# A hybrid decoder layer on eight cores: three barriered stages against an interleaved order with a transposed residual

## The chip, the cores and the metric

The kernel runs on the 8 cores of one Trainium2 chip. Each core computes one of the 8 sequences of the batch, 4096 tokens of 1024 channels, and no core talks to another. The time is that of the slowest core, in microseconds (us) on the device. Within a core, PE (TensorE) multiplies matrices, ACT (ScalarE) and DVE (VectorE) and POOL (GpSimd) do the elementwise work, and SP (SyncE) starts most of the DMAs; each engine works through its own instructions in a fixed order and waits on semaphores.

## What is computed

```python
h = rmsnorm(x, norm1_w); z = h @ w_in            # 1024 -> 5632 columns
q, k, v, xr, yr, ga, gr = split(z)               # 512 512 512 1024 1024 1024 1024
# A: 8 heads of 64; q and k normed; each query sees its own block of 256 keys (causal)
#    and the 3 past blocks whose mean key it likes best; bias by distance; softmax
o_attn = moba_attention(qh, kh, vh, rel_bias)
# B: conv over 4 tokens, then a gated linear recurrence over the sequence
xr = causal_depthwise_conv(xr, conv_w, conv_b)
hr = rg_lru(xr, ...)                             # r, i = sigmoid(block-diagonal 64x64)
o_rnn = hr * gelu(yr)
merged = sigmoid(ga + b) * (o_attn @ w_proj_attn) + sigmoid(gr + b) * (o_rnn @ w_proj_rnn)
x = x + merged @ w_out
x = x + square(relu(rmsnorm(x, norm2_w) @ w_ff1)) @ w_ff2
```

## The kernel before, in words

The kernel is written as a list of operations with the tiles that they read and write (class `Prog`). A planner gives every operation an estimated cost, plays the list through engine by engine, and writes out for each engine the order in which its instructions stand; semaphores follow from the tiles. `P.barrier()` cuts the list in three: behind a barrier every engine waits for all that came ahead of it, DMAs included, and the SBUF space (one arena) is laid out afresh. All instructions are issued from one line (L422), so groups of rows are told apart by their shapes. Tokens are worked in 8 chunks of 512 (`NCH`), each of 4 tiles of 128.

Stage 1 is q, k, v and attention. `frontend` norms a tile (square, Ln and Exp on ACT, one DVE pass) and transposes it on PE into hT. `FE(c)` multiplies hT with the q, k, v columns (24 matmuls of 128x512 a tile), norms q and k, and transposes them head by head. k of all heads (64 rows and 16 rows of block indicators) and v stay in SBUF. `GM(c)` scores each query against the key means of the blocks, takes the third largest with MAX8 and writes a mask of 0 or -30000 into 16 further rows of q, so that the score matmul adds it. `ATT(c, bl)` works on 256 queries of a head at a time: for each pair of key tiles two score matmuls (80x128 by 80x256), one Exp of 512 columns on ACT into PT, and four products with V (128x65). The order is attention of a chunk with `FE` and `GM` of the next put behind its first four heads. x, on SP, is loaded behind the table of biases, which goes through DRAM and back.

Stage 2 is everything from the RNN branch to the residual. Its weights (RNN input, gates, projections, output) are loaded by POOL DMAs that cast fp32 to bf16, and hT and the attention output come back from DRAM. `rnnA`, `rnnB`, `rnnC` are worked two column tiles at a time (`rnn_pair`): conv on DVE, two block-diagonal matmuls, Tanh and Exp and Sqrt on ACT, the scan on DVE, with GeLU built from Square, Tanh and two DVE passes. `rnn_pair` of chunk c+1 stands between the eight `gating` steps of chunk c, then comes the output projection with the residual, token-major, to DRAM.

Stage 3 is the MLP. All of its weights, 16 MB in bf16, are loaded into SBUF by POOL DMAs behind the barrier. `FEC` norms and transposes the tiles of a chunk with `frontend`; 32 groups of 8 matmuls with Relu (ACT) and a square (DVE or POOL) follow, then per token tile two groups of 32 matmuls for W2.

## Time and profile of the kernel before

| | us |
|---|---|
| median of 3 runs | 2813.45 |
| lowest, highest | 2812.91, 2818.64 |
| profiled execution: span of the slowest core | 2811.1 |
| spans of the 8 cores | 2786.8 to 2811.1 |
| PE busy | 2471.3 |
| ACT busy | 1581.7 |
| DVE busy | 1139.7 |
| POOL busy | 297.1 |

Busy time counts an engine's instructions without waits. The granted clock is the share of TensorE's full 2.4 GHz that it was given in a stretch; 1.00 is full, and 0.75 is a mix of its two levels, 2.4 and 1.2 GHz.

### The profile page before, as it was taken

Reading aid. Unit: us, or ns where it says so; the run is one execution under the profiler, and the core shown is the slowest. Engines: PE = TensorE matmul, PEld = TensorE weight load, DVE = VectorE, ACT = ScalarE, POOL = GpSimd, SP = SyncE. Lnnn points to the kernel's source line nnn. Section 1 sums busy time; section 2 is a strip of 40 time slices with the busy share of each in tenths; the row PEclk is TensorE's granted clock in tenths of the full one; section 3 lists DMA queues with packets and bytes.
Section 4 is the critical chain, followed back from the end, with each engine's and each line's share of the span. In section 5 each row is a group of like instructions: output and inputs, shape, how many; then the busy total and the mean of one; then the engine's idle time right before and its main releaser. Section 6 shows DMA issues by size and latency. Waiting matters only on the chain.

```text
span 2811.1 us, 48678 instructions; the slowest of 8 cores (2786.8 to 2811.1 us)
## 1 busy us (share of the span) xinstructions
PE 2471.3 (88%) x16534; PEld 1254.3 (45%) x16722; DVE 1139.7 (41%) x2276; ACT 1581.7 (56%) x2753; POOL 297.1 (11%) x279
## 2 busy tenths in 40 slices
PE   2778888889899746999999999956999999999999
PEld 0445655656565412444444444422444444444444
DVE  2565553342321135777777777321222122121221
ACT  0557867879799737888898889232122131231320
POOL 2000000000000012222222222120001010010110
PEclk9999989989999978999999999977999999999999
DMA  7111101010100194012211220297211211112111
GB/s 121 61 54 54 39 31 54 2 54 6 43 2 10 41 161 73 31 53 83 68 39 60 83 68 23 83 179 136 75 46 45 83 38 61 60 37 84 38 38 53
DMA packets 63373, 166.53 MB, mean 59 GB/s; under 512 B 6883, under 2 KB 27532, under 8 KB 60940
## 3 DMA queue, kind: packets, MB, share of 16 engines
q1 hardware_dynamic: 34428, 129.60, 14.2%
q0 software_dynamic: 28704, 33.82, 8.2%
q8 instruction: 139, 2.28, 0.3%
q14 instruction: 102, 0.84, 0.1%
HBM read 151.07 MB, written 46.15 MB: 70 GB/s over the span
## 4 chain that ended last, share of the span: by engine, by line
PE 78%; DVE 7%; ACT 5%; issue 5%; DMA 3%; another core or an unknown queue 1%; POOL 0%; DVEq 0%; ACTq 0%; SPq 0%; POOLq 0%
PE bank L422 78%; DVE arena L422 7%; ACT arena L422 5%; DMA arena<-w_in 1%; DMA arena<-x 1%; DMA arena<-out 1%; ACT L422 0%; DMA arena<-scr_w 0%; DMA arena<-pvec 0%; POOL arena L422 0%; DVEq L247 0%; DMA scr_w<-arena 0%; DMA out<-arena 0%; ACTq L247 0%
## 5 line engine op out<-in xcount | busy, mean ns | idle before, releaser
L422 PE MATMUL bank<-arena 128*128 128x512 bf16 (+8 forms) x16534 | 2471.3, 304 | 335.9 <-DVE arena L422 148.9
L422 PEld LDWEIGHTS bank<-arena 128*128 128x128 bf16 (+4 forms) x16722 | 1254.3, 100 | 1552.4 <-issue 572.1
L422 ACT ACTIVATE arena<-bank 128x512 bf16<-128x512 f32 (+2 forms) x1472 | 763.5, 781 | 694.9 <-PE bank L422 689.4
L422 ACT ACTIVATE arena<-arena 128x512 f32<-128x512 f32 (+4 forms) x578 | 343.8, 599 | 147.3 <-DVE arena L422 50.5
L422 DVE SCALAR_TENSOR_TENSOR arena<-arena 128x512 f32<-128x512 f32 (+2 forms) x321 | 278.5, 870 | 273.6 <-ACT arena L422 259.0
L422 DVE TENSOR_TENSOR arena<-arena 128x512 bf16<-128x512 f32 (+2 forms) x324 | 204.7, 632 | 327.5 <-ACT arena L422 318.1
L422 POOL TENSOR_TENSOR arena<-arena 128x512 bf16<-128x512 f32 x176 | 212.4, 1207 | 1177.1 <-ACT arena L422 457.3
L422 DVE TENSOR_TENSOR arena<-bank,arena 128x512 bf16<-128x512 f32 (+2 forms) x154 | 92.8, 621 | 372.4 <-PE bank L422 347.9
L422 ACT ACTIVATE arena<-bank,arena 128x512 f32<-128x512 f32 (+1 forms) x288 | 202.5, 733 | 62.5 <-PE bank L422 40.0
L422 DVE SCALAR_TENSOR_TENSOR arena<-arena,bank 128x512 f32<-128x512 f32 x256 | 171.9, 678 | 101.5 <-PE bank L422 62.0
L422 ACT COPY arena<-bank 128x1024 bf16<-128x1024 bf16 (+1 forms) x128 | 103.0, 805 | 186.0 <-PE bank L422 164.7
L422 ACT ACT_TABLE_LOAD x127 | 162.9, 1283 | 67.9 <-DVE arena L422 36.3
L422 DVE RECIPROCAL arena<-bank 128x1 f32<-128x1 f32 x256 | 33.5, 163 | 326.1 <-PE bank L422 325.1
L427 POOL DMA_DIRECT2D arena<-w_in x11 | 9.9, 920 | 956.9 <-DMA scr_o<-arena 956.0
L422 DVE TENSOR_REDUCE arena<-arena 128x16 f32<-128x1024 f32 (+1 forms) x47 | 73.1, 1555 | 71.0 <-ACT arena L422 71.0
L422 DVE TENSOR_TENSOR_SCAN arena<-arena 128x512 f32<-128x512 f32 x64 | 82.9, 1295 | 4.8 <-DVE arena L422 0.5
L422 DVE COPY arena<-bank 16x1024 bf16<-16x1024 bf16 (+3 forms) x97 | 57.8, 596 | 44.8 <-PE bank L422 44.2
L422 POOL TENSOR_SCALAR arena<-arena 128x512 f32<-128x512 f32 x64 | 43.1, 674 | 249.0 <-ACT arena L422 249.0
L422 DVE TENSOR_SCALAR arena<-bank,arena 128x64 bf16<-128x64 f32 x256 | 61.8, 279 | 2.4 <-DVE arena L422 0.6
L422 DVE COPY arena<-arena 128x3 f32<-128x3 f32 (+1 forms) x192 | 40.5, 211 | 50.5 <-ACT arena L422 34.0
L422 DVE SCALAR_TENSOR_TENSOR arena<-bank,arena 128x512 f32<-128x512 f32 x64 | 43.8, 685 | 29.3 <-PE bank L422 29.3
L422 ACT CAST arena<-arena 128x512 bf16<-128x512 f32 x64 | 39.2, 612 | 9.4 <-DVE arena L422 9.1
(18 smaller groups left out, 118.4 us busy)
## 6 DMA issues: line engine op xcount, KB each, us to landing
arena<-x SPq DMA_DIRECT2D x64, 512.0 KB, 4.2
out<-arena SPq DMA_DIRECT2D x64, 512.0 KB, 2.9
arena<-out SPq DMA_DIRECT2D x64, 512.0 KB, 4.3
arena<-w_ff POOLq DMA_DIRECT2D x16, 1024.0 KB, 77.0
arena<-w_in POOLq DMA_DIRECT2D x11, 1024.0 KB, 30.6
scr_h<-arena SPq DMA_DIRECT2D x8, 1024.0 KB, 4.9
arena<-scr_h SPq DMA_DIRECT2D x8, 1024.0 KB, 4.8
scr_o<-arena SPq DMA_DIRECT2D x8, 512.0 KB, 3.0
```

Of the source, the lines that this page charges most:

```text
L422: return P.add(eng, lambda e, m=meth, kw=kw: getattr(e, m)(**kw), reads, writes, cost=cost, fam=fam)
L427: return P.add(q, lambda e, kw=kw: e.dma_start(out=out, in_=in_, **kw), reads, writes, dsem=dsem, cost=(1200.0 if q == 'gpsimd' else 60.0) ...
```

## The change

The three stages are re-cut, the barriers go, and a new planner orders the whole program at once. The new planner takes at each moment, for each engine, the earliest-written operation that is ready by its own estimates; space is still laid out by stage, but an operation waits only for the users of the bytes that it takes over.

- Stage 1 is q, k, v alone. The reciprocal root of each norm is a power on POOL in place of Ln and Exp. q and k are transposed two heads at a time. hT, q, k and v are stored to DRAM, and the RNN and gate weights are loaded meanwhile, one load a tile.
- Stage 2 is the RNN branch, four column tiles at a time with GeLU in one instruction, with `GATE1` of the chunk before: both gates, the RNN projection, and its product with its gate. The attention gate (`t1_s`) and the gated RNN term (`rm_s`) go to DRAM in fp32. POOL DMAs cast the MLP weights from DRAM to DRAM into bf16 (`WCAST`).
- Stage 3 runs the rest. Attention works on 512 queries at a time, loads the keys and values of a head for each chunk (`KVLOAD`), and its units are spread between the dense units (gating, output projection, MLP) of the chunk before. MLP weights are re-read from DRAM in slabs of 1 MB for each chunk, four slabs deep. x and the result are held with channels on partitions (`xT`, `outT`, transposed on the host), so that the second norm is a column sum over ones on PE and needs no transposes. Scores have three PSUM banks, V products two, and all else three.

```diff
-            P.barrier()
+            if eng == "tensor":
+                nmov = fsize(kw["rhs"]) if "rhs" in kw else 128
+                c_ = max(nmov / 2.4 + 2.6, 28.0)
...
+                    if kw.get("op", None) == ALU.pow:
+                        c_ = nel * 135.0 + 800.0
...
+        load_x(0)
+        dma("sync", nw, nw_d, "c0b", [], ["nw"])
...
+        for j in range(3):
+            dma("gpsimd", wqkv[j], wqkv_d[j].rearrange("p (a b) -> p a b", a=8), "wqkv%d" % j, [], ["wqkv%d" % j])
...
+        abank = ring([1, 2, 3, 4, 5, 6])
+        hbank = ring([0])
+        tbank = ring([7])
...
+            op("gpsimd", "tensor_scalar", [sk], [sk], out=ssq[s], in0=ssq[s], scalar1=EPS, scalar2=None, op0=ALU.add)
+            op("gpsimd", "tensor_tensor", [sk, "mhalf"], [sk], out=ssq[s], in0=ssq[s], in1=mhalf, op=ALU.pow)
...
+        FEn(0)
+        for t in range(NT):
+            if t + 1 < NT:
+                FEn(t + 1)
+            FEq(t, FEm(t))
+            if t >= 4 and wB:
+                w_, src, nm = wB.pop(0)
+                dma("gpsimd", w_, src.rearrange("p (a b) -> p a b", a=8), nm, ["hT%d" % (t % NHT)], [nm])
+            if t == 6:
+                bias_table()
...
+        for s in range(NCH):
+            for g in range(2):
+                RNN(s, g)
...
+                if s > 0:
+                    for m in range(4 * g, 4 * g + 2):
+                        GATE1(s - 1, m)
+                RNN2(s, g)
+                if s > 0:
+                    for m in range(4 * g + 2, 4 * g + 4):
+                        GATE1(s - 1, m)
+                for _ in range(2):
+                    WCAST("orn:%d" % ((s * 8 + 4 * g) % NORN))
...
+        SB = [0, 1, 3]
+        OB = [2, 4]
+        DB = [5, 6, 7]
+        def gbank():
+            b = DB[gctr[0] % 3]
+            gctr[0] += 1
+            return b
...
+                        op("tensor", "matmul", ["kTr%d" % ks, "kTr%d:E" % ks] + qk, ["B%d" % sb], tag="S", out=bankf[sb][:, 0:nq],
+                           lhsT=kTr[ks][0:80, kt * 128:(kt + 1) * 128], rhs=qT[s][0:80, h, q0:CH], start=True, stop=bias is None)
...
+                        op("scalar", "activation", ["B%d" % sb], ["PT%d" % pi], out=PT[pi][:, 0:nq], in_=bankf[sb][:, 0:nq], func=AF.Exp, fam="expln")
+                        for qt in range(q0 // 128, 4):
+                            op("tensor", "matmul", ["PT%d" % pi, "Vr%d" % ks], ["B%d" % ob], tag="AV", out=bankf[ob][:, qt * 65:(qt + 1) * 65],
...
+                    dma("sync", t1r[r], t1_s[c, m], "t1r%d" % r, ["t1_s%d_%d" % (c, m)], ["t1r%d" % r])
+                    dma("sync", rmr[r], rm_s[c, m], "rmr%d" % r, ["rm_s%d_%d" % (c, m)], ["rmr%d" % r])
+                    b = gbank()
...
+                        op("tensor", "matmul", ["ss", "onesf"], ["B%d" % b2], tag="nrm", out=bankf[b2], lhsT=onesf, rhs=ss, start=True, stop=True)
...
+        extend(gating(0))
+        extend(outproj(0))
+        for c in range(NCH):
+            nx = c + 1 < NCH
+            extend(W1(c, 0))
+            extend(W2(c, 0))
+            extend(W1(c, 1))
+            w2 = W2(c, 1)
+            if nx:
+                marks[c + 1] = len(dense)
+                extend(gating(c + 1))
+                o_ = outproj(c + 1)
+                extend(o_[0:4])
+                extend(w2[0:4])
+                extend(o_[4:8])
+                extend(w2[4:8])
...
+            at = attention(c)
...
+            inject.setdefault(prev, []).append(lambda c=c: (QLOAD(c), GM(c)))
+            for i in range(prev, end):
+                acc += dense[i][0]
+                goal = tot * min(1.0, acc / (dt_tot * 0.92))
```

## Rows read from the trace of the kernel before

**Rows 1.** The page: span, and busy time of PE.

```profile
span 2811.1 us, 48678 instructions; the slowest of 8 cores (2786.8 to 2811.1 us)
...
PE 2471.3 (88%) x16534; PEld 1254.3 (45%) x16722; DVE 1139.7 (41%) x2276; ACT 1581.7 (56%) x2753; POOL 297.1 (11%) x279
```

**Rows 2.** Windows by stage: stretch, length, busy us (instructions), granted clock, DMA share, GB/s.

```profile
0.00:66.40 66.40, 10.64 (x19) 2.94 (x20) 13.26 (x16) 4.44 (x9) 17.01 (x8) 1.00 0.73 125
66.40:970.30 903.90, 786.36 (x8864) 495.52 (x8896) 357.80 (x1055) 705.00 (x1435) 0.00 (x0) 0.94 0.10 32
970.30:1110.70 140.40, 65.11 (x212) 23.79 (x217) 59.80 (x101) 73.84 (x102) 28.57 (x31) 0.73 0.80 137
1110.70:1825.90 715.20, 701.74 (x3175) 314.05 (x3240) 502.04 (x831) 566.17 (x791) 155.18 (x145) 1.00 0.18 58
1825.90:1960.20 134.30, 74.36 (x327) 33.04 (x332) 24.80 (x30) 36.91 (x67) 23.40 (x26) 0.75 0.96 165
1960.20:2811.10 850.90, 833.10 (x3940) 384.96 (x4020) 181.95 (x243) 195.38 (x350) 72.90 (x70) 1.00 0.16 54
```

**Rows 3.** Timeline of PE at the handovers: start, length, work, idle before and its releaser.

```profile
999.93 9.28 PE L422 MATMUL bank<-arena 128*128 128x512 bf16 x31 [29.66 <-DMA arena<-w_in]
...
1931.61 1.86 PE L422 MATMUL bank<-arena 128*128 128x512 bf16 x4 [6.78 <-DMA arena<-w_ff]
```

**Rows 4.** Timeline of DVE at the end: sums of output half tiles, 32 matmuls each.

```profile
2779.74 0.69 DVE L422 TENSOR_TENSOR arena<-bank,arena 128x512 f32<-128x512 f32 x1 [6.21 <-PE bank L422]
...
2807.37 0.69 DVE L422 TENSOR_TENSOR arena<-bank,arena 128x512 f32<-128x512 f32 x1 [6.21 <-PE bank L422]
```

**Rows 5.** Windows, columns as in rows 2: attention alone, late in its stage.

```profile
840.00:910.00 70.00, 67.71 (x874) 39.39 (x871) 9.10 (x44) 69.86 (x145) 0.00 (x0) 1.00 0.03 10
```

**Rows 6.** Timeline of PE: sixteen transposes in a row.

```profile
75.21 1.21 PE L422 MATMUL bank<-arena 128*64 128x128 bf16 x16 [1.47 <-DVE arena L422]
```

**Rows 7.** Groups by form, whole run: operation, shape, count, busy, mean ns, idle before.

```profile
L422 DVE MAX8 arena<-arena 128x8 f32<-128x16 f32 x208 | 36.6, 176 | 18.2 <-DVE arena L422 1.8
...
L422 PE MATMUL bank<-arena 128*128 128x512 f32 x8 | 8.2, 1127 | 27.8 <-DMA arena<-scr_w 27.8
...
L422 DVE TENSOR_TENSOR arena<-arena 128x128 f32<-128x128 f32 x26 | 7.5, 290 | 2.0
```

**Rows 8.** DMA issues: count, KB each, median us from issue to landing.

```profile
arena<-x SPq DMA_DIRECT2D x64, 512.0 KB, 4.2
out<-arena SPq DMA_DIRECT2D x64, 512.0 KB, 2.9
...
arena<-scr_h SPq DMA_DIRECT2D x8, 1024.0 KB, 4.8
...
arena<-w_proj_attn POOLq DMA_DIRECT2D x1, 1024.0 KB, 11.2
```

**Rows 9.** Groups by form, whole run: passes of the q, k, v stage, and POOL.

```profile
L422 POOL TENSOR_TENSOR arena<-arena 128x512 bf16<-128x512 f32 x176 | 212.4, 1207 | 1177.1 <-ACT arena L422 457.3 <-PE bank L422 396.5 <-DVE arena L422 323.3
...
L422 DVE SCALAR_TENSOR_TENSOR arena<-arena 128x1024 bf16<-128x1024 f32 x64 | 82.1, 1283 | 174.8 <-ACT arena L422 161.9 <-issue 12.9
...
L422 DVE TENSOR_TENSOR arena<-bank,arena 128x512 bf16<-128x512 f32 x64 | 41.2, 685 | 24.4 <-ACT arena L422 24.4
...
L422 DVE TENSOR_REDUCE arena<-arena 128x16 f32<-128x1024 f32 x32 | 38.9, 1217 | 52.1 <-ACT arena L422 52.1
...
L422 DVE TENSOR_REDUCE arena<-arena 64x8 f32<-64x2048 bf16 x15 | 34.2, 2278 | 19.0 <-ACT arena L422 19.0
...
L422 DVE COPY arena<-bank 64x1024 bf16<-64x1024 bf16 x32 | 21.8, 682 | 8.0 <-PE bank L422 7.9
```

**Rows 10.** Groups by form, PE in the attention stage (110.6 to 970.3): scores, V products.

```profile
L422 PE MATMUL bank<-arena 80*128 80x256 bf16 x2048 | 391.8, 282 | 14.4 <-ACT arena L422 11.0 <-DVE arena L422 2.2
L422 PE MATMUL bank<-arena 128*128 128x65 bf16 x4224 | 278.6, 196 | 18.1 <-ACT arena L422 9.1 <-DVE arena L422 2.8
```

**Rows 11.** Timeline of PE: the last V products of the attention stage.

```profile
966.33 0.28 PE L422 MATMUL bank<-arena 128*128 128x65 bf16 x4 [0.21 <-ACT arena L422]
```

More of the change, by code:

```diff
@@ new lines, in emit @@
+                if ds is not None:
+                    assert dq.setdefault(ds, e) == e
+                    dcount[ds] = dcount.get(ds, 0) + 16
+                    sig[i] = ("d:" + ds, dcount[ds])
+                elif has[i]:
+                    c += 1
+                    sig[i] = ("e:" + e, c)
+        names = sorted(set(s[0] for s in sig if s is not None))
+        pos = sorted(range(n), key=lambda i: (self.t0[i], i))
+        known = {e: {} for e in self.ENGS}
+        carried = [None] * n
@@ new lines, in emit @@
+        waits = [()] * n
+        for i in pos:
+            o = ops[i]
+            kn = known[o.eng]
+            want = {}
+            srcs = {}
+            for j in deps[i]:
+                if skip(j, i):
+                    continue
+                s, v = sig[j]
+                if v > want.get(s, 0):
+                    want[s] = v
+                    srcs[s] = j
+            w = []
+            for s in sorted(want, key=lambda s: -self.t1[srcs[s]]):
+                if kn.get(s, 0) >= want[s]:
+                    continue
+                w.append((s, want[s]))
+                kn[s] = want[s]
+                for s2, v2 in carried[srcs[s]].items():
+                    if v2 > kn.get(s2, 0):
+                        kn[s2] = v2
+            waits[i] = w
+            c = dict(kn)
+            own = "e:" + o.eng
+            if o.dsem is None and sig[i] is not None:
+                c[own] = sig[i][1]
+            carried[i] = c
@@ L364, in build_nc @@
     cG_d = dt_in("c_G", [33, 384])
[L365 removed]
+    cE_d = dt_in("c_E", [16, S], BF16)
     cm_d = dt_in("c_mtab", [128, 768])
[L367 to L371 removed]
@@ new lines, in build_nc @@
+        QLOAD(0)
+        GM(0)
+        dma("gpsimd", wpa, wpa_d.rearrange("p (a b) -> p a b", a=4), "wpa", [], ["wpa"])
+        dma("gpsimd", wo, wo_d.rearrange("p (a b) -> p a b", a=8), "wo", [], ["wo"])
+        at0 = attention(0)
+        for m in range(8):
+            for _, f in at0[m * 4:m * 4 + 4]:
+                f()
+            GATE1(NCH - 1, m)
+        for _, f in at0[32:]:
+            f()
+        for _ in range(3):
+            WLOAD()
+        dense = []
+        marks = {}
@@ new lines, in build_nc @@
+        inject = {}
+        prev = 0
+        for c in range(1, NCH):
+            end = marks[c]
+            at = attention(c)
+            tot = sum(w for w, _ in at)
+            dt_tot = sum(w for w, _ in dense[prev:end])
+            acc = 0.0
+            k = 0
+            inject.setdefault(prev, []).append(lambda c=c: (QLOAD(c), GM(c)))
+            for i in range(prev, end):
+                acc += dense[i][0]
+                goal = tot * min(1.0, acc / (dt_tot * 0.92))
+                while k < len(at) and (sum_ := sum(w for w, _ in at[:k])) < goal:
+                    inject.setdefault(i + 1, []).append(at[k][1])
+                    k += 1
+            while k < len(at):
+                inject.setdefault(end, []).append(at[k][1])
+                k += 1
+            prev = end
@@ L997, in build_nc @@
+        for i in range(len(dense) + 1):
+            for f in inject.get(i, ()):
+                f()
+            if i < len(dense):
+                dense[i][1]()
+        P.emit(nc, ["out%d_%d" % (c, dt_) for c in range(NCH) for dt_ in range(8)])
+        st.pop().close() if len(st) > 1 else None
+        build_nc.stats = (len(P.ops), P.n_sems, P.n_waits, P.end, {k: round(v / 1e3) for k, v in P.busy.items()}, pA_peak, pB_peak, p2_peak)
+        build_nc.prog = P
     return nc
 def _prep_inputs(inputs):
-    f = lambda a: np.ascontiguousarray(np.asarray(a, dtype=np.float32))
```

1661 lines of the change are left out of this document (812 added, 849 removed).

## Prediction

> **What bounds the kernel now.** I read the page first: TensorE is busy for 2471.3 of 2811.1 us [rows 1], so at most 340 us are idle, and a change that keeps its work can win little more than those. Then the busy time by stage, cut where the PE timeline shows the handovers [rows 2, 3]. The reader is to see three things there. The last two stages proper (RNN with gating, 1110.7 to 1825.9, and MLP, from 1960.2) hold PE busy for 701.7 of 715.2 and 833.1 of 850.9 us at a granted clock of 1.00: nothing is to be won in them. The attention stage leaves 903.9 - 786.4 = 117.5 us idle, at a clock of 0.94, so its work also runs slower than it could. And three stretches are mostly empty: the start (66.4 us, 10.6 busy), and the two handovers at the barriers (140.4 with 65.1 busy and 134.3 with 74.4 busy, at 0.73 and 0.75). In the first handover PE waits 29.7 us for weights, in the second 7 us at a time [rows 3]. Losses: 55.8 + 117.5 + 75.3 + 13.5 + 59.9 + 17.8 = 339.8 us.
>
> **What PE has to do afterwards.** A 128x512 matmul takes 27.63/128 = 0.2159 us (the four last output tiles, 2779.74 to 2807.37 [rows 4]). The change leaves their number: q, k, v 768, RNN input 1024, its gate blocks 128, merge gates 1024, the two projections 512 + 256, output 512, MLP 2048 + 2048; together 8320, 1796 us. Attention keeps its columns too: 67,584 score columns for each head before (256 queries at a time) and after (512 at a time, the four tiles on the diagonal 512 to 128 wide), plus 64,512 bias columns in all; 605,184 columns at 0.2159/512 are 255 us. The 4224 products with V stay. Their price comes from the end of the attention stage, where nothing else runs: 67.71 us of PE for 145 exps are 0.467 us for a pair of key tiles [rows 5], less 0.216 for 512 score columns, over four products: 0.063 us each, 265 us. Transposes fall from 1408 to 672 (q and k two heads at a time, masks all heads at once, no transposes ahead of the MLP because the residual is kept transposed): at 1.21/16 = 0.076 us [rows 6] 51 us. New are eight fp32 column sums over ones for the second norm, 1.127 us each by the fp32 row [rows 7], 9 us; 104 small block-score matmuls at not over 0.063 are 6.5. Sum: 2383 us at full clock.
>
> **Start.** Before, x sits on SP behind the bias table, and q starts at 66 us. After, x is the first load, and the bias table moves behind tile 6. What is late next is the weights of v, third on POOL's queue: a 1024 KB load there took 11.2 us when little else was queued [rows 8], so three are some 34 us; a few q and k matmuls fit ahead. Idle: 28 us.
>
> **Stage 1, q, k, v.** A tile is 24 x 0.2159 + 16 x 0.076 = 6.4 us of PE. DVE has 1.28 (norm) + 0.68 (copy of h) + 1.22 (two sums) + 2 x 0.69 + about 0.4 (q out) + half of a key sum, 2.28/4 = 0.57 [rows 9]: 5.5 us, just under. Ahead of the q and k scaling stands something new, a power on POOL (1 and 16 elements) in place of Ln and Exp on ACT, with two small adds. No POOL power is in the trace. From below it is free (hidden); from the other side the nearest POOL row, 512 elements in 1.21 us [rows 9], is far away; the change's own planner prices it at 135 ns an element plus 0.8, so 3.9 us a tile. Both hide under 6.4 us, and six banks let two tiles be in flight; I take 10 us of waits, and twice the planner's price, 7.8 us and the adds, would make POOL the bound at about 9 and cost 80 us. At the 0.94 of the old attention stage the 214 us of PE cost 14 more. The 22 weight loads moved onto POOL's queue stand one a tile behind these powers; they are needed only after the stage.
>
> **Stage 2, RNN and gates.** Step 0 has no gates of an earlier chunk beside it. Before, RNN of chunk 0 took 1110.7 - 999.9 = 110.8 us in four dependent pairs [rows 2, 3]; now there are two groups of four: about 56 us for 31 us of PE, 25 idle, and 10 more for its clock by the 0.73 to 0.75 of the handovers. The seven further steps have 336 matmuls, 72.5 us; the old stage lost 1.9% [rows 2], so 10 us over 508. ACT sheds one pass (GeLU in one instruction) and DVE two; not bound before, so worth nothing. The 128 new stores of gate terms stand on SP alone, hidden behind 508 us.
>
> **Into stage 3.** No barrier any more, and weights wait in DRAM as bf16, cast by POOL DMAs during stage 2. But the projection of chunk 7 waits for its last RNN chain, and it shares banks with attention of chunk 0: 18 us, against 59.9 before.
>
> **Stage 3.** 1053 us of dense matmuls and 540 of attention share PE. ACT has 0.482 us for an exp [rows 5], 1152 of them at most 555 us, and some 200 us of the rest: far from bound. DMA re-reads 16 MB of MLP weights a chunk, and at most 32 MB with keys, values, gate terms and x; at 1024 KB in 4.8 us [rows 8] that is under 154 of some 200 us, so hidden. Every score must go through exp before its V product, and PE works in order: in the old stage PE idled 14.4 + 18.1 us ahead of these two [rows 10]; I take 32 again, with 512-wide matmuls as better cover and a planner that knows the same latencies.
>
> One place I expect to wait: the seven chunk borders. All dense units, and the block mask of the next chunk, take banks 5, 6, 7 in one program-order ring. The mask (issued first) is a DVE chain of eight MAX8 at 0.176 and three passes at 0.29, 2.3 us and hops, so 10.5 us for four tiles [rows 7]. Behind it in the ring stand gating, output projection, and only then the second half of W2 that was put there as cover. Gating also waits on SP's reloads: two buffers, each round a load (under 4.2 us), 0.69 and 1.21 [rows 8, 9]. PE's other cover is the next chunk's attention, which needs the mask through eight more small DMAs on SP (landing as the 2.9 us store [rows 8], some 5.5 us with their issue). From the last W1 matmul: 10.5 - 3.5 (the mask starts two units early) + 5.5 - 3.5 (gating matmuls that fit) = 9 us each, 63 us. Bounds: 0 if attention of the old chunk is left over, and 30 us each if gating's four reload rounds (6.5 us each) stay bare too.
>
> **Tail**: 2811.1 - 2807.4 = 4 us as before [rows 1, 4].
>
> **Sum.** 2383 + 28 + 10 + 14 + 25 + 10 + 10 + 18 + 32 + 63 + 4 = 2597 us of span, against 2811.1. The median before is 2813.45, 2.4 above its span, so 2600 us.
>
> **Rivals.**
> (a) Slower: PE waits for exp inside stage 3. Place: the V products of 1152 units; the fixed order can put a product too close behind its score. The trace shows bare waits of 0.21 us ahead of four products where no other work is left [rows 11]; the worst is a whole exp, 0.482. At 0.35, halfway, 1152 x 0.35 = 403 in place of 32: 2971 us. It decides from (2813 - 2600 + 32)/1152 = 0.21 us a unit. Against it: only 18.1 us of such idle in 1088 pairs [rows 10]. For it: the planner prices a V product at 30 ns where the row gives 63, so its picture of stage 3 is off.
> (b) The borders cost 30 us each: 2600 - 63 + 210 = 2747.
> (c) Power on POOL bounds stage 1: 2600 + 80 = 2680.
> (d) Clock: with more engines busy beside PE, stage 3 gets the 0.94 of the old attention stage, 1600 us x 0.064: 2702. Against it: 1.00 where ACT and PE were both full [rows 5].
> (e) All cover works, borders and V products free: 2600 - 95 = 2505.
> (f) The change does not do what it says, attention runs in lumps after all: then ACT sets 0.482 in place of 0.467 a unit, 17 us: 2617, inside the forecast's own range.
>
> Rows give 1.00, the 2.4 GHz level, in the MLP stage [rows 2], and 0.2159 us a matmul. The Trainium skill ("TensorE: Matmul & The Clock Gate", Seeing it yourself, the note on the peak-current limiter) states 13/16 of that when several cores of a die run dense matmuls; by that the sum of matmuls would be 2383 x 16/13 = 2933 and the time 3150. All eight cores run the MLP here at 1.00, so the trace does not agree, and I leave it within the chance of (d).
>
> **Chances.** Forecast (2540 to 2660) 0.53, (f) 0.05, (e) 0.10, (b) 0.12, (c) 0.06, (d) 0.03, (a) 0.11. The range leaves out (a) and a little below (e): 2500 to 2770. Faster by over 0.2% (about what a measurement of this kernel can tell from no change) in all but (a): 0.87 after 0.02 for a sum of (b), (c) and (d) that just meets the old time; slower 0.11.
>
> **What would show it.** Right: PE busy near 2400 us and over 95% from some 330 us to the end; no empty handover near 850 us; dips of about 10 us at seven borders, released by DVE or DMA. Wrong: PE idle spread through stage 3 and released by ACT (a); borders of 30 us (b); stage 1 much over 240 us with DVE waiting on POOL (c); a clock under 1.00 while PE is full (d).

## The result and the profile after

The changed kernel takes 2650.2 us (median) against 2813.8 us for the kernel before, run beside it: a ratio of 0.941, with an interval of 0.939 to 0.943, so 164 us less. The forecast was 2600 us, in a range of 2500 to 2770. Some executions were lengthened by a lower clock on one die (core 0 in the profiled one of e2: PE busy for 100.00 of the 100 us from 2500 at a granted clock of 0.81), so the ratios, the times of the runs below and e2's rows, which are core 4's, leave these out. Differences between kernels are taken from their ratios to the kernel before, times 2814 us.

The page of the profiled execution (span 2647.7 us), beside [rows 1]: span and busy time of each engine.

```profile
span 2647.7 us, 43842 instructions; the slowest of 8 cores (2624.2 to 2647.7 us)
...
PE 2369.7 (90%) x14810; PEld 1131.8 (43%) x14810; DVE 1093.7 (41%) x1946; ACT 1287.8 (49%) x2313; POOL 729.4 (28%) x593
```

The windows by stage, columns as in [rows 2]: start, stage 1 (q, k, v), step 0 of the RNN, its steps 1 to 7, the handover, and the rest of stage 3.

```profile
0.00:45.50 45.50, 15.27 (x71) 7.22 (x72) 11.18 (x25) 8.68 (x16) 10.94 (x19) 1.00 0.89 208
45.50:285.00 239.50, 207.84 (x1252) 103.65 (x1251) 168.15 (x269) 107.03 (x187) 150.53 (x142) 0.94 0.93 195
285.00:345.70 60.70, 39.47 (x171) 16.73 (x169) 42.09 (x61) 40.51 (x61) 40.64 (x31) 0.83 0.37 61
345.70:900.00 554.30, 514.11 (x2314) 227.43 (x2314) 395.30 (x562) 368.68 (x546) 336.14 (x238) 0.98 0.39 93
900.00:1035.00 135.00, 89.62 (x489) 39.65 (x490) 33.84 (x86) 33.53 (x68) 11.76 (x10) 0.76 0.64 178
1035.00:2647.70 1612.70, 1503.41 (x10519) 737.15 (x10517) 443.18 (x948) 729.36 (x1437) 179.37 (x156) 0.96 0.46 144
```

Length less PE's busy time is the idle time: 30.2, 31.7, 21.2, 40.2, 45.4 and 109.3 us, 278.0 together. Busy time multiplied by the granted clock is what the same work would take at full clock; what is left of the busy time is lost to the clock. The clock is often low while PE waits and has nothing to lose, so the product is taken in windows of 1 us (over the six rows above it would put 111 us on the clock). The two profiles and the forecast then stand side by side, rounded:

| us | before [rows 2] | forecast | after |
|---|---|---|---|
| PE work at full clock | 2393 | 2383 | 2292 |
| lost to the clock | 79 | 24 | 78 |
| PE idle | 340 | 190 | 278 |
| span | 2811 | 2597 | 2648 |

The reader is to see that the total came within 2% by errors that cancel, which is luck. The forecast took its gain from idle time and clock, 205 us of 214. In fact the work shrank by 101 us and the idle time by 62, and the clock gave back 1. Some of what is called work here is waiting that PE's rows do not show as idle; e7_price tells how.

Where the idle time is, by groups of instructions over the whole run (busy us, mean ns, then PE's or the engine's idle time ahead of them and what ended it):

```profile
L461 PE MATMUL bank<-s_Vr,s_PT 128*128 128x65 bf16 x4224 | 313.7, 195 | 23.9 <-ACT s_PT L461 21.7 <-DVE s_otm L461 0.8
L461 PE MATMUL bank<-s_qT,s_kTr 80*128 80x512 bf16 x960 | 311.7, 387 | 9.7 <-DMA s_qT<-s_mskT 7.5 <-ACT s_PT L461 1.2 <-DVE s_t_0 L461 0.4
...
L461 POOL TENSOR_SCALAR s_rr<-s_rr 128x512 f32<-128x512 f32 x64 | 140.1, 2202 | 0.3 <-POOL s_rr L461 0.3
L461 POOL TENSOR_TENSOR s_ssq<-s_ssq,s_mhalf 128x16 f32<-128x16 f32 x32 | 98.7, 3085 | 3.9
...
L461 PE MATMUL bank<-s_oT,s_wpa 128*128 128x512 bf16 x256 | 91.0, 492 | 44.0 <-DVE s_t1r L461 43.4 <-DVE s_mskT L461 0.5
...
L461 PE MATMUL bank<-s_cvb,s_wbda 128*128 128x512 bf16 x64 | 25.6, 403 | 41.6 <-POOL s_cvb L461 21.4 <-DVE s_xr L461 20.2
...
L461 PE MATMUL bank<-s_identb,s_maskb 128*128 128x128 bf16 x32 | 7.9, 247 | 37.2 <-DVE s_maskb L461 37.2
```

The idle time ahead of V products and scores, the first two lines, is small (33.6 us, where [rows 10] had 32.5); 22.9 of it ended with an exponential on ACT, 7.5 with the mask's stores. The large waits are the gating sums (44.0 us until `t1r` is ready), the RNN's block products (41.6) and the mask (37.2).

One chunk border in windows of 5 us, columns as in [rows 2], late in stage 3:

```profile
2215.00:2220.00 5.00, 3.88 (x25) 1.82 (x23) 2.12 (x7) 1.79 (x3) 1.04 (x1) 1.00 0.32 88
2220.00:2225.00 5.00, 1.07 (x10) 0.59 (x10) 4.20 (x32) 0.00 (x0) 0.00 (x0) 0.64 0.49 190
2225.00:2230.00 5.00, 4.20 (x11) 1.28 (x12) 3.08 (x16) 0.00 (x0) 0.37 (x1) 0.50 0.00 0
2230.00:2235.00 5.00, 4.49 (x21) 1.70 (x20) 1.15 (x3) 1.21 (x3) 0.90 (x1) 0.83 0.05 16
2235.00:2240.00 5.00, 1.00 (x11) 0.42 (x10) 0.28 (x1) 1.83 (x4) 0.00 (x0) 0.85 0.45 140
2240.00:2245.00 5.00, 4.45 (x28) 2.31 (x29) 2.13 (x4) 2.11 (x4) 1.26 (x1) 0.50 0.64 207
```

PE runs dry twice, at 2220 and at 2235, and each time the granted clock falls to the lower level (0.50 is 1.2 GHz) in the stretch behind it. The timeline of PE names the two waits, the mask and then `t1r`; the lines of SP show why the second comes, the reload of `t1r` issued behind the eight mask stores of 5.09 us (start, length, work, idle before and releaser).

```profile
2221.49 0.27 PE L461 MATMUL bank<-s_identb,s_maskb 128*128 128x128 bf16 x1 [1.81 <-DVE s_maskb L461]
...
2231.10 5.09 SPq L466 DMA_DIRECT2D s_qT<-s_mskT  x8
2236.28 1.00 SPq L466 DMA_DIRECT2D s_t1r<-t_s  x1
...
2240.55 0.59 PE L461 MATMUL bank<-s_oT,s_wpa 128*128 128x512 bf16 x1 [4.55 <-DVE s_t1r L461]
```

### The profile page after: what moved, and what is told of

Its sections match the earlier page's. It is cut to its first block, busy times and chain, and to the rows that moved or that the text cites. A ratio compares the mean times of both kernels' runs of the same rounds, so it can differ in the third digit from the quotient of the medians.

```text
span 2647.7 us, 43842 instructions; the slowest of 8 cores (2624.2 to 2647.7 us)
## 1 busy us (share of the span) xinstructions
PE 2369.7 (90%) x14810; PEld 1131.8 (43%) x14810; DVE 1093.7 (41%) x1946; ACT 1287.8 (49%) x2313; POOL 729.4 (28%) x593
## 4 chain that ended last, share of the span: by engine, by line
PE 69%; issue 8%; DMA 8%; DVE 6%; POOL 3%; ACT 3%; SPq 2%; DVEq 0%; ACTq 0%; POOLq 0%
PE bank L461 69%; DMA q_s<-s_qst 2%; DMA s_t1r<-t_s 2%; SPq L466 2%; POOL s_ssq L461 2%; DVE s_cv L461 1%; DVE s_ii L461 1%; DMA s_xs<-x 1%; DMA s_x1T<-xT 1%; DMA outT<-s_x1T 1%; POOL s_orn L461 1%; ACT L461 1%; ACT s_PT L461 1%; DMA t_s<-s_t_0 1%; DMA rm_s<-s_t_0 1%
## 5 line engine op out<-in xcount | busy, mean ns | idle before, releaser
L461 ACT ACTIVATE s_PT<-bank 128x512 bf16<-128x512 f32 (+3 forms) x1152 | 568.2, 566 | 485.8 <-PE bank L461 482.8
L461 PE MATMUL bank<-s_h2T,s_wsl 128*128 128x512 bf16 x2048 | 520.9, 379 | 2.0 <-ACT s_rl L461 1.3
L461 PE MATMUL bank<-s_uT,s_wsl 128*128 128x512 bf16 x2048 | 508.6, 381 | 4.8 <-DVE s_x1T L461 4.8
L461 PEld LDWEIGHTS bank<-s_Vr,s_PT 128*128 128x128 bf16 x4224 | 251.3, 98 | 284.4 <-issue 223.4
L461 PE MATMUL bank<-s_qT,s_kTr 80*128 80x512 bf16 (+3 forms) x1152 | 359.9, 369 | 9.7 <-DMA s_qT<-s_mskT 7.5
L461 PE MATMUL bank<-s_Vr,s_PT 128*128 128x65 bf16 x4224 | 313.7, 195 | 23.9 <-ACT s_PT L461 21.7
L461 ACT ACTIVATE s_rl<-bank 128x512 f32<-128x512 f32 x256 | 152.8, 597 | 295.7 <-PE bank L461 294.0
L461 PEld LDWEIGHTS bank<-s_uT,s_wsl 128*128 128x128 bf16 x2048 | 187.1, 98 | 186.1 <-issue 14.2
L461 PEld LDWEIGHTS bank<-s_h2T,s_wsl 128*128 128x128 bf16 x2048 | 183.7, 98 | 165.2 <-issue 3.9
L461 PE MATMUL bank<-s_wqkv,s_hT 128*128 128x512 bf16 x768 | 190.6, 397 | 10.3 <-DVE s_hbias L461 6.8
L461 POOL TENSOR_SCALAR s_rr<-s_rr 128x512 f32<-128x512 f32 x64 | 140.1, 2202 | 0.3 <-POOL s_rr L461 0.3
## 6 DMA issues: line engine op xcount, KB each, us to landing
s_xs<-x SPq DMA_DIRECT2D x32, 512.0 KB, 10.3
```

The costliest lines, as they stand in the source:

```text
L461: return P.add(eng, lambda e, m=meth, kw=kw: getattr(e, m)(**kw), reads, writes, cost=c_, lat=lat, fam=fam, tag=tag or (writes[0] if write ...
```

## The experiments

Twelve runs. The first five take one suspected wait away each, and e5 two of them; the next three ask where TensorE's work went; the rest put the cures together (e9_best is the kernel of e12_best_again).

| kernel | ratio to before | interval | against the changed kernel, us |
|---|---|---|---|
| changed kernel | 0.9408 | 0.9390 to 0.9426 | |
| e1_minmax | 0.9271 | 0.9257 to 0.9285 | -39 |
| e4_fewer_loads | 0.9342 | 0.9327 to 0.9358 | -19 |
| e8_handover | 0.9366 | 0.9351 to 0.9381 | -12 |
| e2_mask_early | 0.9251 | 0.9235 to 0.9266 | -44 |
| e13_w2_alone | 0.9219 | 0.9199 to 0.9239 | -53 |
| e5_w2_between | 0.9012 | 0.8992 to 0.9031 | -111 |
| e3_in_turn | 1.0379 | 1.0362 to 1.0397 | +273 |
| e7_price | 0.9593 | 0.9576 to 0.9610 | +52 |
| e10_price15 | 0.9399 | 0.9357 to 0.9441 | -3 (unclear) |
| e12_best_again | 0.8754 | 0.8735 to 0.8773 | -184 |
| e11_best15 | 0.8733 | 0.8714 to 0.8752 | -190 |

### e1_minmax: the clamp on POOL

```diff
-                op("gpsimd", "tensor_scalar", ["rr%d" % r], ["rr%d" % r], out=rr[r], in0=rr[r], scalar1=1.0, scalar2=-0.25, op0=ALU.min, op1=ALU.mult)
+                op("gpsimd", "tensor_scalar", ["rr%d" % r], ["rr%d" % r], out=rr[r], in0=rr[r], scalar1=1.0, scalar2=0.0, op0=ALU.min, op1=ALU.max)
...
-                op("scalar", "activation", ["rr%d" % r], ["rr%d" % r], out=rr[r], in_=rr[r], func=AF.Sqrt, scale=1.0, bias=0.25)
+                op("scalar", "activation", ["rr%d" % r], ["rr%d" % r], out=rr[r], in_=rr[r], func=AF.Sqrt, scale=-0.25, bias=0.25)
```

> One POOL pass of the RNN, minimum then multiply by -0.25 (2.20 us in the changed kernel), becomes minimum then maximum with 0, the form of the old kernel (0.67 us there); the factor goes into the scale of the square root behind it. Theory: this pass stretches the RNN chain, 64 x 1.5 = 98 us of POOL, and DVE passes beside it are slow too; PE's bare time in steps 1 to 7 (40.2 us in 345.7 to 900) falls to 10 to 20, the handover behind it (45.4) by some 8, since the mask copies stand behind the last RNN chain on DVE: 2650 to about 2615. Rival: PE's fixed order and its buffers set these waits, POOL is idle 40% of that stage anyway; then the pass is shorter and the time stays within 5 us.

Measured: 2608.9 us, 39 to 41 below the changed kernel, a little more than the theory. The group on POOL, and then the RNN steps 1 to 7 as a window (columns as in [rows 2]):

```profile
L461 POOL TENSOR_SCALAR s_rr<-s_rr 128x512 f32<-128x512 f32 x64 | 38.5, 617 | 0.3 <-POOL s_rr L461 0.3
```

```profile
345.70:860.00 514.30, 503.40 (x2310) 225.77 (x2310) 365.36 (x555) 361.58 (x541) 247.99 (x237) 1.00 0.41 100
```

The pass went from 2202 to 617 ns, and steps 1 to 7 from 554.3 us with 40.2 idle at a clock of 0.98 to 514.3 with 10.9 idle at 1.00. So the excess wait of these steps is this one instruction, at the head of the chain from the gates to the scan. The handover behind it did not get shorter (51.8 us idle from 860 to 995).

### e4_fewer_loads: the transfers of stage 1

Twelve of the 22 weight loads that went out one a tile during q, k, v (gates and RNN projection, which are needed only in step 1) go out behind the first RNN group.

```diff
-            if t >= 4 and wB:
+            if t >= 4 and len(wB) > 12:
...
+                if s == 0 and g == 0:
+                    for i in range(12):
+                        w_, src, nm = wB.pop(0)
+                        dma("gpsimd", w_, src.rearrange("p (a b) -> p a b", a=8), nm, ["cvb%d" % (i // 3)], [nm])
```

> The twelve loads of gate and RNN projection weights leave stage 1 and are issued behind the first RNN group; the ten RNN loads stay. Theory: stage 1 waits for DMA, whose engines are busy 0.93 of 45.5 to 285 (x lands after 10.3 us, against 4.2 before); with 12 of 22 weight loads gone PE's 31.7 us of bare time there fall to 15 or less, and the time by 10 to 15. Rival: the waits are the latency of POOL's power (3.09 us for 16 elements) ahead of the scaling; then stage 1 stays, and the time may grow by up to 10 because gates of chunk 0 wait for their weights.

Measured: 2627.9 us, 19 to 22 below, so more than the theory's 10 to 15. The window of stage 1, which is now over 15 us earlier:

```profile
45.50:270.00 224.50, 208.37 (x1289) 104.79 (x1287) 173.63 (x280) 112.03 (x195) 150.15 (x140) 0.98 0.86 186
```

Idle time 16.1 us where the changed kernel had 31.7, at a clock of 0.98 where it had 0.94, and the DMA share down from 0.93 to 0.86. POOL is as busy as before, so its powers are not what held stage 1; the transfers are. (Issuing the twelve loads also took POOL 0.6 us each, which its busy time leaves out; the run does not part these 7 us from the transfers.) The longest wait of the changed kernel's stage 1 shows how: DVE waits for a store of q to give its buffer back, 28.0 us from issue to landing, and PE stands for 9.7 us behind it. No wait of PE over 2.5 us is left in e4's stage 1.

```profile
162.29 0.42 DVE L461 COPY s_qst<-bank 128x512 bf16<-128x512 bf16 x1 [10.77 <-DMA q_s<-s_qst]
```

### e8_handover: the way into stage 3

The mask of chunk 0, which comes from a table alone, is built in RNN step 1 with two small buffers of its own; loads of `xT` and weight slabs wait until a few gating units have run.

```diff
-        GM(0)
+        for h in range(NH):
+            dma("sync", qT[0][64:80, h, :], mskT0[h * 16:(h + 1) * 16, :], "mk%d" % h, ["mskT0"], ["qT0:m%d" % h])
...
-                    dma("sync", x1T[:, xi, :], xT_d[dt_ * 128:(dt_ + 1) * 128, c * CH:(c + 1) * CH], "xl%d" % xi, [], [xk])
+                    dma("sync", x1T[:, xi, :], xT_d[dt_ * 128:(dt_ + 1) * 128, c * CH:(c + 1) * CH], "xl%d" % xi, ["mT:%d" % (dt_ // 2)] if c == 0 else ["h2T:0"], [xk])
```

> Edit: the mask of chunk 0, which comes from a table alone, is built in the second RNN step instead of behind the last RNN chain on VectorE; of the twelve loads of the transposed residual that went out ahead of the first gating load, and three of the four 1 MB weight slabs, all but a few wait until gating units 0 to 7 have run. Theory (the handover's idle time, 45 us at a clock of 0.76 between 900 and 1035, is 11 us of waiting for the mask and 11 to 13 of waiting for a first t1 load that stands in the queues behind 6 MB, and the clock falls because of them): 18 to 28 us below the changed kernel, 2622 to 2632. Rival (PE then waits at the next thing that is late there, the end of the last RNN chain that the last gate terms need, and the weight slabs that now come later): 6 us or less, 2644 or more, the idle time ahead of the s_orn or the W1 products.

Measured: 2632.1 us; 18 less by the times, 12 by the ratios, so at or below the lower edge of the theory and above the rival. The handover's window, and the group of the mask transposes with PE's wait ahead of them:

```profile
900.00:1035.00 135.00, 103.33 (x597) 48.94 (x604) 45.40 (x98) 51.82 (x96) 30.85 (x22) 0.86 0.61 182
```

```profile
L461 PE MATMUL bank<-s_identb,s_maskb 128*128 128x128 bf16 x32 | 8.1, 253 | 24.7 <-DVE s_maskb L461 24.7
```

The mask wait of 12.5 us is gone (37.2 to 24.7) and 8 us of the gating wait (44.0 to 35.9); the window's idle time fell only from 45.4 to 31.7, because new waits stand in it, 7.0 us of them on loads of `kTr`, where none was. And outside the window the cure has a price of its own. In RNN step 1 PE now stands for 11.6 us, since the early mask takes a bank and its copy waits on DVE behind the passes of the convolution:

```profile
361.50 2.72 PE L461 MATMUL bank<-s_hTb,s_wga 128*128 128x512 bf16 x6 [11.63 <-DVE s_mskT L461]
```

Both causes were real, but the wait for the mask was mostly moved to another stage, not removed.

### e2_mask_early and e13_w2_alone: the two waits of a chunk border

e2 issues the mask of the next chunk, tile by tile, nine to three dense units ahead of the border. e13 leaves it at the border, and puts one W2 unit of the present chunk behind every second gating unit of the next.

```diff
-            inject.setdefault(prev, []).append(lambda c=c: (QLOAD(c), GM(c)))
+                inject.setdefault(prev - 12, []).append(lambda c=c: QLOAD(c))
+                for tl in range(TPC):
+                    inject.setdefault(prev - 9 + 2 * tl, []).append(lambda c=c, tl=tl: GM(c, [tl]))
```

```diff
-                extend(gating(c + 1))
+                g_ = gating(c + 1)
...
+                for i in range(4):
+                    extend(g_[2 * i:2 * i + 2])
+                    extend(w2[i:i + 1])
```

> The loads of q and the four mask tiles of the chunk after next move from the chunk border to 12 and 9 dense units ahead of it, one tile every second unit, from chunk 2 on. Theory: the mask chain holds the ring of three banks and the next chunk's attention, and its eight small DMAs stand on SP ahead of gating's reloads; six of seven borders lose 11.2 us of PE each and some clock, and 6 to 9 of those come back: 2650 to 2595 to 2615. Rival: gating's reloads alone end the border, two buffers a round; then PE still waits for them and no more than 2 us a border come back, 2640.

> Edit: only the W2 units between the gating units, as in e5_w2_between; the masks stay at the border, as in the changed kernel. e5 gained 117 us against the changed kernel, 45 of them with the early masks alone. Theory A (two separate waits at a border, which add): 2650 - 72 = 2578, 2570 to 2586. Rival B (the mask stands ahead of the gating sums in the ring of banks, so that its 10 us stay bare whatever follows, and the W2 units help only once it is early): 2600 to 2630, with the idle time ahead of the mask transposes and block scores as in the changed kernel (37 and 13 us).

Measured: e2 2605.2 us (44 less, as its theory had it), e13 2593.4 us (53 less; theory A said 72, rival B 20 to 50). PE's groups with their idle time, first e2, then e13:

```profile
L461 PE MATMUL bank<-s_oT,s_wpa 128*128 128x512 bf16 x242 | 78.4, 445 | 32.1 <-DVE s_t1r L461 30.4 <-DVE s_mskT L461 0.5 <-DVE s_top L461 0.4
...
L461 PE MATMUL bank<-s_identb,s_maskb 128*128 128x128 bf16 x32 | 7.5, 236 | 14.6 <-DVE s_maskb L461 14.6
```

```profile
L461 PE MATMUL bank<-s_oT,s_wpa 128*128 128x512 bf16 x256 | 85.4, 450 | 14.7 <-DVE s_t1r L461 13.9 <-DVE s_mskT L461 0.5
L461 PE MATMUL bank<-s_identb,s_maskb 128*128 128x128 bf16 x32 | 8.0, 250 | 37.2 <-DVE s_maskb L461 37.2
```

Each removes its own wait and leaves the other: the mask's falls from 37.2 to 14.6 in e2 and stays at 37.2 in e13, the gating's from 44.0 to 14.7 in e13. So the mask at the head of the ring does not make the W2 units useless, as rival B had it; two waits stand at a border one behind the other. (Of what is left, 12.2 of the 14.6 us and 11.5 of the 14.7 stand at the handover.) Theory A priced the second from e5 less e2, and there it is worth 67, not 53.

### e5_w2_between: both

> Edit: the early mask of e2_mask_early, and in addition one W2 unit (16 products, 3.5 us) of the present chunk after every second gating unit of the next, so that the two-buffer reloads of t1 and rm have PE work to hide under. Theory (what is left of a border in e2 is the wait of the gating sums for their reloads, 32.1 us ahead of the s_oT,s_wpa products in e2, some 13 of them at the handover and so about 19 at seven borders): 10 to 18 us below e2, 2587 to 2595. Rival (three banks in the ring hold the W2 units back as well, or the W2 units moved up are missed as cover for the RMS statistics at the end of the output projection): no gain against e2, 2605 +- 4, with the idle time turning up ahead of the W1 products.

Measured: 2533.3 us, 111 to 117 below the changed kernel and far below both theory and rival. The two cures add up to 97, and some 14 more come only together. A chunk from one column sum to the next, in the changed kernel and in e5 (windows, columns as in [rows 2]):

```profile
1839.30:2065.30 226.00, 212.48 (x1645) 107.08 (x1645) 58.96 (x135) 122.10 (x243) 23.05 (x20) 0.96 0.49 148
```

```profile
1781.20:1990.40 209.20, 206.01 (x1644) 106.22 (x1644) 58.99 (x135) 122.59 (x244) 23.32 (x20) 0.99 0.51 160
```

Idle time falls from 13.5 to 3.2 us, and PE's own busy time by 6.5, although it has the same to do. In windows of 1 us, 5.3 of these busy us are lost to the clock in the changed kernel and 1.6 in e5, which is 3.7 of the 6.5; waits that PE's records hide (see e7_price) are 3.3 and 1.6, which is 1.7 more. Over the whole run idle time falls by 71 us (278.0 to 206.7), the loss to the clock by 28 (78 to 50) and the rest of the busy time by 17. My expectation counted idle microseconds, and each of them here brought 0.4 more by the clock.

### e3_in_turn: attention ahead of the dense work

All attention of a chunk stands ahead of the dense units that it was spread among, and their matmuls wait for its end.

```diff
+            inject.setdefault(prev, []).extend(f for _, f in at)
+            inject[prev].append(lambda c=c: gate.__setitem__(0, ["oT%d:%d" % (c % 2, i) for i in range(4)]))
...
-                        op("tensor", "matmul", ["mT:%d" % i for i in range(8)] + ["wo"], ["B%d" % b], tag="op", out=bankf[b], lhsT=wo[:, kt, dt_ * 128:(dt_ + 1) * 128],
+                        op("tensor", "matmul", ["mT:%d" % i for i in range(8)] + ["wo"] + gate[0], ["B%d" % b], tag="op", out=bankf[b], lhsT=wo[:, kt, dt_ * 128:(dt_ + 1) * 128],
```

> The overlap of the change undone, the rest kept: in stage 3 all attention of a chunk stands ahead of the dense work of the chunk before, and the dense matmuls wait for its end. Theory (the prediction's own case f): ACT then sets 0.482 us a unit in place of PE's 0.467, 17 us over seven chunks, and the mask chain and the loads in front of each attention are bare, 7 x 10 more: about 2730. Rival: the overlap carries the gain; then the time goes back to the old kernel's 2813 or above.

Measured: 2920.4 us, 273 above the changed kernel and slower than the kernel before: the theory fell, by a factor of three, and the rival held. The middle of an attention stretch, as a window and on PE's timeline (start, length, work):

```profile
1925.00:2000.00 75.00, 71.17 (x760) 34.31 (x759) 3.64 (x12) 72.90 (x154) 0.00 (x0) 1.00 0.31 76
```

```profile
1961.81 0.28 PE L461 MATMUL bank<-s_Vr,s_PT 128*128 128x65 bf16 x4
1961.92 0.38 PE L461 MATMUL bank<-s_qT,s_kTr 80*128 80x512 bf16 x1
1962.30 0.28 PE L461 MATMUL bank<-s_Vr,s_PT 128*128 128x65 bf16 x4
1962.41 0.38 PE L461 MATMUL bank<-s_qT,s_kTr 80*128 80x512 bf16 x1
```

A unit takes 0.49 us here, and ACT is full (72.9 of 75): the V products wait for their exponentials. That agrees with the 0.482 I had used; the other half of the comparison was wrong. I thought that PE needs 0.467 for a unit wherever it stands. Among dense work it needs much less, as the changed kernel's timeline shows, and that is what e3 gives up:

```profile
1930.70 0.60 PE L461 MATMUL bank<-s_uT,s_wsl 128*128 128x512 bf16 x2
1931.14 0.28 PE L461 MATMUL bank<-s_Vr,s_PT 128*128 128x65 bf16 x4
1931.26 0.60 PE L461 MATMUL bank<-s_uT,s_wsl 128*128 128x512 bf16 x2
1931.69 0.28 PE L461 MATMUL bank<-s_Vr,s_PT 128*128 128x65 bf16 x4
```

From the start of four V products to the next work is 0.12 us, 0.030 each, and the two wide matmuls take 0.43, two times 0.216: nothing is lost. A unit is worth 0.216 + 0.12 = 0.336 us of PE in the mix, against 0.49 alone. By the profiles (span 2920.1 us, PE busy for 2512.5) idle time is 130 us more than in the changed kernel (the largest waits are 53.9 us ahead of the output projection and 37.5 for the mask's stores) and the loss to the clock 39 more; the other 103 us of busy time are this wait for exponentials.

### e7_price and e10_price15: the order on PE

Only the planner's price of a V product, 29.7 ns in the changed kernel, is altered.

```diff
-                c_ = max(nmov / 2.4 + 2.6, 28.0)
+                c_ = 63.0 if nmov == 65 else max(nmov / 2.4 + 2.6, 28.0)
```

> Edit: only the planner's price of a V product (65 columns), from 29.7 to the 63 ns that PE took in the trace of before; the program is the same, each engine's order changes. The planner's own end goes from 2465 to 2591 us by it, so its picture of the attention is 126 us off in the changed kernel. Theory (the orders on PE are set by which sums are ready, and the waits come from POOL's clamp, the queue of loads and the borders, none of which this price touches): 2642 to 2656. Rival (the orders were planned for a PE that is too fast in the attention, so scores are issued too late ahead of their V products): the 33 us of waits on scores and V products go by half or more, 2630 or less.

Measured: 2696.6 us, 52 slower by the ratio. Theory and rival both fell: with the price that I had read from the trace of before, the plan got worse. The same chunk as above, and PE's timeline in it:

```profile
1849.30:2088.10 238.80, 226.36 (x1643) 106.77 (x1644) 58.87 (x135) 121.94 (x243) 23.05 (x20) 0.96 0.46 140
```

```profile
1949.97 0.28 PE L461 MATMUL bank<-s_Vr,s_PT 128*128 128x65 bf16 x4
1950.09 0.38 PE L461 MATMUL bank<-s_uT,s_wsl 128*128 128x512 bf16 x1
1950.46 0.28 PE L461 MATMUL bank<-s_Vr,s_PT 128*128 128x65 bf16 x4
```

ACT in e7 at this place, and then PE at a place of the same form in the changed kernel:

```profile
1948.24 2.08 ACT L461 ACTIVATE s_PT<-bank 128x512 bf16<-128x512 f32 x4
```

```profile
1929.81 0.38 PE L461 MATMUL bank<-s_qT,s_kTr 80*128 80x512 bf16 x1
1930.03 0.28 PE L461 MATMUL bank<-s_Vr,s_PT 128*128 128x65 bf16 x4
```

Idle time (12.4 us) and loss to the clock (7.7) are near those of the changed kernel (13.5 and 5.3); the work is not, 218.7 us against 207.1. Where two groups of V products are parted by one wide matmul, that one takes 0.37 us from 1950.09 to 1950.46, though it only has 0.216 to do. I counted such places in the timelines of this chunk: 104 in e7, 0.337 us each; 42 in the changed kernel, 0.264 each. The excess over 0.216 is 12.6 us against 2.0, which is most of the 12.8 us by which the chunk is longer.

The reason stands in ACT's line. The last of its four exponentials ends at 1948.24 + 2.08 = 1950.32, and the V products that read it start 0.14 us later: PE waits for the exponential. Exponentials and V products stand in the same order in both traces, so each product can be set against its own exponential: no product starts less than 0.143 us after the end of it. Of e7's 104 places 101 stand at full clock, 94 of these last over 0.26 us, and behind all 94 the products start 0.143 to 0.146 us after their exponential. Where it ends in time, a single wide matmul is not stretched: it takes 0.22 us from 1929.81 to 1930.03, with four V products on either side there too, and 0.215 to 0.222 at the 18 places of both chunks at full clock whose exponential had ended over 0.15 us before. So the weight loads that the expectations of e10_price15 and e11_best15 blame are not the cause.

PE's rows do not show this wait as idle. The record of a wide matmul lasts 0.38 us, while the next one can start 0.216 after it, so that up to 0.16 us of a wait behind it is booked as busy. I added up, over the V products that start within 0.147 us of their exponential, what their start is later than the columns ahead of them ask: 21 us are hidden so in the changed kernel and 75 in e7, and these 54 account for the 52 that e7 lost. Why the plan leaves less room between a score and its V products when they are priced dearer is open.

> Edit: only the planner's price of a V product, as in e7_price, but from 29.7 to 15 ns. In the order that comes of it only 146 groups of four V products are parted by a single wide product, against 259 in the changed kernel and 524 in e7_price. Theory (e7_price is slow because one wide product between two groups of V products can't hide their weight loads: there the wide one takes 0.33 us instead of 0.216, 47 us over all; in the changed kernel that excess is 10 us): 4 to 12 us below the changed kernel, 2638 to 2646. Rival (a wrong price harms in itself, or the effect is some other shift of the order that goes with the price in a straight line): 2675 or more by the first, 2620 or less by the second.

Measured: 2636.6, 2638.3 and 2665.3 us, ratio 0.940 (0.936 to 0.944). Both rivals are out (2657 at most and 2633 at least, by the interval); whether the expected 4 to 12 us are there can't be told.

### e9_best, e12_best_again and e11_best15: together

> Edit: e1_minmax, e4_fewer_loads, e5_w2_between and e8_handover together. Theory (each takes away a wait of another stage, so they add): 2650 - 41 - 20 - 57 - 23 = 2509, 2495 to 2530, PE idle below 130 us. Rival (the waits shadow each other: what the faster RNN stage gains is lost again at the handover, what the borders gain is lost to waits on scores): two thirds of the sum, 2545 to 2560.

Measured: 2460.8 us, in a single execution, below even the first theory, for the most part by what e5 had brought beyond its own expectation. Measured again:

> Edit: none against e9_best (min and max, early masks, W2 between the gating units, fewer loads in stage 1, handover); measured again beside the others for an interval. Expected: 2455 to 2470, the gains of its parts added and some 40 us more, as the one profile of e9_best showed.

Measured: 2464.7 us (2459.8 to 2471.4), ratio 0.875. The single gains of e1, e4, e8 and e5 sum to 39 + 19 + 12 + 111 = 181 us, and together they bring 184. They add, within their intervals, as waits in different stages should. The page:

```profile
span 2463.6 us, 43874 instructions; the slowest of 8 cores (2441.3 to 2463.6 us)
...
PE 2305.2 (94%) x14810; PEld 1122.5 (46%) x14810; DVE 1062.9 (43%) x1946; ACT 1286.7 (52%) x2314; POOL 632.8 (26%) x593
```

Idle time is 158.4 us, against 278.0, and 33 us are lost to the clock, against 78.

> Edit: e9_best with the price of 15 ns, which leaves 78 single wide products between groups of V products instead of 207. Theory (weight loads without cover): 5 to 12 us below e9_best. Rival (there is nothing left to gain, since ACT's exponentials then come too late for the V products): level with e9_best or up to 10 us above, with more idle time ahead of the V products.

Measured: 2457.5 us, ratio 0.873 (0.871 to 0.875) against 0.875 (0.874 to 0.877): in the expected direction, with 9.7 us of waits ahead of the V products where e12 has 9.8, but the intervals overlap. The waits hidden behind records are 6 us against 10.

## Why the prediction came out as it did

**Work.** This step failed, to the good: 2383 forecast, 2292 found. The term was the V products, 4224 at 0.063 us. I took that from [rows 5], a stretch where ACT was busy for 69.86 of 70 us; the 0.467 us of a pair was the pace of ACT, not PE's price. In that stretch 112 of 123 groups of V products start 0.143 to 0.147 us behind the end of an exponential. The products themselves take 0.030 (127 us, not 265); four in a row last 0.28 us in [rows 11] as in the changed kernel. I counted the planner's 30 ns against it, in rival (a); it was right. By the working of the forecast with 0.030 the sum is 1796 + 255 + 127 + 66 = 2244, with the 21 us of hidden waits 2265; the other 27 are open. Against the kernel before, 101 us of work are gone: 736 transposes at 0.076 are up to 56 of them, and the hidden waits, counted behind the nearest end of an instruction on ACT, fell from 74 us to 21.

**Clock.** This failed the other way: 24 forecast, 78 found. I charged the clock in two stages only. The handover lost 18 us by it, and the rest of stage 3 39, nearly all behind borders, where the rows of 5 us show 0.50. e5 gave much of it back, with nothing else changed than the waits.

**Start**: 28 forecast, 30.2 measured, but not by the wait that was priced, so the number is luck. The weights of v landed at 31.6 us, near the 34 I had, and no long wait of PE is for them. PE stood for 16.05 us until the identity matrix of the transposes had landed, for 5.8 until the second tile was normed, and for 6.8 because the copy of that tile stood on DVE behind an operation that waited for a small load:

```profile
33.59 0.17 DVE L461 SCALAR_TENSOR_TENSOR s_qkw<-s_qkcol 128x1 f32<-128x1 f32 x1 [6.26 <-DMA s_qkcol<-qk_col]
```

**Step 0 of the RNN**: 25 idle forecast, 21.2 measured, 19.2 of them one wait for a convolution. The 10 for its clock were too much: 2.4 us were lost while PE was busy.

**Stage 1**: 10 idle forecast, 31.7 measured; the clock of 0.94 was right, 10 us lost for the 14. Power on POOL was priced well (3085 ns for 16 elements and 632 for one, against the 3.9 us a tile taken), and did not bind: POOL was busy for 150.5 of 239.5 us. What I had dismissed did, the 22 weight loads ("they are needed only after the stage"): they share the DMA engines, 0.93 busy, with the loads of x (10.3 us each, where [rows 8] had 4.2) and the stores of h, q, k and v. e4 shows it.

**Steps 1 to 7**: 10 idle forecast, 40.2 measured. I had scaled the old stage's 1.9% and did not price the instruction on POOL that heads the chain; a POOL pass of that shape took 674 ns in the kernel before, and min with a multiplication took 2202. With e1 the measured figure is 10.9.

**Into stage 3**: 18 forecast. The window of the handover, which also holds the first border (9), has 45.4. Not the banks and not the last chain alone: the mask of chunk 0 stood on DVE behind that chain (12.5 us by e8, which paid 11.6 for it in step 1), and the first `t1r` load behind 6 MB of loads that were not yet needed (10.9 us, 5.8 in e8).

**Exponentials**: 32 forecast, 33.6 measured ahead of the same two groups. The figures are not the same thing: 22.9 us ended with an exponential, and 21 more of such waits are hidden in the busy time. With some 44 us in place of the 403, rival (a), the only one on the other side, is out.

**Borders**: the mechanism was right to the queue: mask, then the mask's stores on SP, then the reloads. The size was off. Idle time in the rest of stage 3 is 109.3 us where the forecast had 99 - 9 = 90, and most of the 39 us of clock belong here too. Removing the two waits was worth 111 us, not 63. Rival (b), 210, was too much; (e), where all cover works, is about what e5 then reached by other orders.

**Other rivals.** (c) is out, stage 1 lasted 239.5 us. (d) was not the place: where PE is full in stage 3 the rows give 1.00; the clock was lost where PE had waited. The Trainium skill ("TensorE: Matmul & The Clock Gate", Seeing it yourself) has a limiter that puts a die with several busy cores at 13/16 of the clock; no such row is in the changed kernel's profile either, while the 0.81 of e2's core 0, given with the result, is that level. (f): attention does run in the mix, and e3 shows what it costs if it doesn't, 273 us rather than 17, of which 130 are idle time.

Of the signs of being right, the dips at the borders came; PE was busy for 91.5% from 345.7 us on, not over 95, and the handover was idle for 45.4 of 135 us.

So the forecast was 50 us short: 88 us too little idle time and 54 too little lost to the clock, less 91 too much work.

## What to carry to other kernels

Before you take an instruction's price from a stretch, look which engine is full there: the V products cost 0.03 us in both kernels, and the 0.063 was ACT's pace. Compare the starts of TensorE's instructions and not only their lengths, since a wait of up to 0.16 us can lie under a record of 0.38. Count a long wait of TensorE at more than its length, since the clock behind it is part of the price (0.4 us for each us in e5). When a change moves work in time, read its transfers and the slow engine at the head of each chain as closely as the bound engine; the three misses on idle time were a load "needed only later", a two-operation pass on POOL, and a queue.

## What the runs showed of the hardware

- A pass of two operations on POOL depends on which they are: 128x512 fp32 with min and max took 617 ns, with min and a multiplication 2202.
- DVE's first pass of the scan chain, 128x512 fp32 with two operations, took 1438 ns in the changed kernel and 1161 with the short clamp on POOL; the nearest shape took about 770 before. POOL is busier beside it now, but no run here takes POOL away, so the cause stays open. A copy of 3 columns into the halo took 695 ns on DVE (242 before, over the copies in both directions), and 683 with the short clamp, so the clamp is not its cause.
- Four V products of 65 columns take 0.12 us from the first start to the next work.
- A 512-column matmul's record lasts 0.38 us and the next can start 0.216 us after it; in e7 it was 0.37 where the next product waited for an exponential, and the page counts that as busy.
- A V product started no less than 0.143 us after the end of the exponential that it reads, in the changed kernel and in e7.
